# TensorE takes a mixer step one dense section ahead of the other engines in the feed-forward parts

## What is computed

```python
h = rmsnorm(x); u = h @ w_in
mix = concat(rglru(u), ssd(u), gated_delta(u), s5(u))   # four recurrent mixers
x = x + mix @ w_out
x = x + cross_attend(rmsnorm(x), mem_k, mem_v)
x = x + (silu(h2 @ w_gate) * (h2 @ w_up)) @ w_down       # h2 = rmsnorm(x), 2816 hidden
y = rmsnorm(x)
```

## Time and profile before

| | |
|---|---|
| median of 3 runs | 3927.91 us (3922.59 to 3929.86) |
| the profiled execution's own time | 3928.61 us |
| its span, first to last instruction | 3926.7 us |
| PE busy | 3555.5 us, 91% |
| PEld busy | 3385.3 us, 86% |
| DVE busy | 2189.3 us, 56% |
| ACT busy | 1349.6 us, 34% |
| mean granted TensorE clock | 0.949 |

### The profile page before, as it was taken

The page is one execution under the profiler, slowest core; times in us unless marked ns, Lnnn a source line. Parts: engine busy times, 40 slices in busy tenths (PEclk is TensorE's granted clock), DMA queues, the critical chain, the costliest instruction groups (busy, mean ns, idle before and its releaser), DMA issues.

```text
span 3926.7 us, 67616 instructions
## 1 busy us (share of the span) xinstructions
PE 3555.5 (91%) x26198; PEld 3385.3 (86%) x26198; DVE 2189.3 (56%) x4725; ACT 1349.6 (34%) x2497; POOL 97.1 (2%) x319
## 2 busy tenths in 40 slices
PE   6779796889879999889999998999998999989998
PEld 6778686678878999889899988899988899989998
DVE  6556754367855665663655572655573655554323
ACT  5553424244534343423332332322332432322101
POOL 2200001000000000000000000000000000000000
PEclk8979897889989999999999999999999999999999
DMA  7767567867686677667566667566668555566776
GB/s 222 235 228 252 191 213 246 240 209 241 234 283 246 245 276 265 249 237 259 194 229 217 211 236 282 188 230 221 217 220 281 187 203 189 204 236 237 250 252 212
DMA packets 370175, 909.58 MB, mean 232 GB/s; under 512 B 34368, under 2 KB 173248, under 8 KB 369472
## 3 DMA queue, kind: packets, MB, share of 16 engines
q1 hardware_dynamic: 369856, 905.26, 67.2%
HBM read 730.56 MB, written 174.57 MB: 231 GB/s over the span
## 4 chain that ended last, share of the span: by engine, by line
PE 49%; issue 19%; DVE 13%; DMA 6%; ACT 6%; DVEq 3%; SPq 2%; POOLq 1%; ACTq 1%; POOL 0%; PEldq 0%; PEld 0%
PE banks L479 14%; PE banks L480 13%; PE banks L481 13%; PE banks L1690 2%; DVE wlo_sb L1175 2%; DMA wlo_sb<-kept_dram 2%; ACT whi_sb L966 1%; DMA kept_dram<-wlo_sb 1%; DVE uc_sb L1267 1%; DVE m_p_sb L2297 1%; DVE m_p_sb L2267 1%; DVE hl_sb L1194 1%; DVE acc_sb L1184 1%; PE banks L1660 1%; DVE rstd_sb L1334 1%
## 5 line engine op out<-in xcount | busy, mean ns | idle before, releaser
L479 PE MATMUL banks<-hh_sb,whi_sb 128*128 128x384 f32 (+1 forms) x3360 | 1154.1, 343 | 98.1 <-DVE wlo_sb L1175 34.8
L480 PE MATMUL banks<-hh_sb,wlo_sb 128*128 128x384 f32 (+1 forms) x3360 | 1120.1, 333 | 0.0
L481 PE MATMUL banks<-hl_sb,whi_sb 128*128 128x384 f32 (+1 forms) x3360 | 1117.9, 333 | 0.0
L479 PEld LDWEIGHTS banks<-hh_sb,whi_sb 128*128 128x128 f32 x3360 | 650.7, 194 | 124.1 <-DVE wlo_sb L1175 43.2
L480 PEld LDWEIGHTS banks<-hh_sb,wlo_sb 128*128 128x128 f32 x3360 | 651.4, 194 | 1.6 <-issue 0.6
L481 PEld LDWEIGHTS banks<-hl_sb,whi_sb 128*128 128x128 f32 x3360 | 649.5, 193 | 0.0
L479 PE MATMUL banks<-g_hi_sb,whi_sb 128*128 128x384 f32 (+2 forms) x1504 | 516.4, 343 | 52.0 <-DVE x_sb L1380 21.5
L481 PE MATMUL banks<-g_lo_sb,whi_sb 128*128 128x384 f32 (+2 forms) x1504 | 501.8, 334 | 0.0
L480 PE MATMUL banks<-g_hi_sb,wlo_sb 128*128 128x384 f32 (+2 forms) x1504 | 501.6, 334 | 0.0
L1380 DVE TENSOR_TENSOR x_sb<-x_sb,banks 128x384 f32<-128x384 f32 (+2 forms) x400 | 201.3, 514 | 290.5 <-PE banks L481 274.7
L479 PEld LDWEIGHTS banks<-g_hi_sb,whi_sb 128*128 128x128 f32 x1504 | 294.9, 196 | 67.4 <-DVE x_sb L1380 25.2
(11 more groups left out here) (447 smaller groups left out, 4843.2 us busy)
## 6 DMA issues: line engine op xcount, KB each, us to landing
whi_sb<-kept_dram SPq DMA_DIRECT2D x504, 512.0 KB, 3.8
wlo_sb<-kept_dram SPq DMA_DIRECT2D x504, 512.0 KB, 4.9
raw_sb<-w SPq DMA_DIRECT2D x176, 512.0 KB, 5.0
kept_dram<-whi_sb SPq DMA_DIRECT2D x112, 512.0 KB, 5.3
kept_dram<-wlo_sb SPq DMA_DIRECT2D x112, 512.0 KB, 6.2
uc_dram<-uc_sb SPq DMA_DIRECT2D x90, 192.0 KB, 2.7
ldb_sb<-x_t SPq DMA_DIRECT2D x64, 192.0 KB, 4.6
plain_sb<-w SPq DMA_DIRECT2D x32, 256.0 KB, 5.0
```

Source lines behind the costliest of these rows:

```text
L479: eng.matmul(out, xh, yh, start=first, stop=False)
L480: eng.matmul(out, xl, yh, start=False, stop=False)
L481: return eng.matmul(out, xh, yl, start=False, stop=last)
```

## The change

`PE_PLAN` is a second plan, for PE alone. For each section `i` of kind `g`, `up` or `d` of a pass other than 0 that has a step behind it, PE takes one of its steps behind section `i - 1`, which is in front of section `i`. The other engines keep `PLAN`. The steps themselves, their waits and the sections are the same.

```diff
@@ -428,6 +428,19 @@
 PLAN = spread_over_windows()
+def ahead_on_pe():
+    plan = list(PLAN)
+    for i in range(1, len(SECS)):
+        if SECS[i].p and PLAN[i] and SECS[i].kind in ("g", "up", "d"):
+            plan[i] -= 1
+            plan[i - 1] += 1
+    return plan
+PE_PLAN = ahead_on_pe()
@@ -2879,11 +2892,11 @@
-        def weave(eng, section, mixer):
+        def weave(eng, section, mixer, plan=PLAN):
             mix = mixer(eng)
             for i in range(len(SECS)):
                 section(eng, i)
-                for _ in range(PLAN[i]):
+                for _ in range(plan[i]):
                     next(mix)
@@ -2892,7 +2905,7 @@
-            weave(pe, pe_section, pe_mixer)
+            weave(pe, pe_section, pe_mixer, PE_PLAN)
```

## The result

| | before | after |
|---|---|---|
| median (lowest to highest), 4 runs each | 3926.34 us (3922.59 to 3929.86) | 4151.98 us (4150.98 to 4161.36) |
| the profiled execution's own time | 3928.61 us | 4152.82 us |
| its span | 3926.7 us | 4150.9 us |
| mean granted TensorE clock | 0.949 | 0.942 |

The changed kernel is slower: the ratio after to before is 1.0584, with an interval of 1.0571 to 1.0596, which is 229 us; the medians lie 226 apart. From the planner on, the file is longer by 13 lines, so L1690 of before is L1703 of after, L2330 is L2343, L2349 is L2362, and so on.

What follows compares the result with a forecast made beforehand. PE was taken to bound the feed-forward parts of passes 1 to 4. Waits 201 - 24.5 given back + 36 clock = 212 us on 3928.6, so 4141, given as 4140 against the median; 8-in-10 range 4050 to 4250.

Steps and rivals of the forecast that it cites:

- Which waits: Of 122 moved steps with another step at section i-1, 106 make PE wait; 16 wait for ACT behind a d, priced at nothing.
- split by pass: The 122 steps with a step at i-1: 26 in each of passes 1 to 3, 44 in pass 4.
- Price of one: Each of 106 PE waits: section end to end of the needed DVE or ACT instruction, plus 0.15 us restart; 201 us.
- the rival of 4059 to 4100: Prices are smaller: the long steps shrink, giving 4059 us, or up to 4100 if only some do; chance 0.17.
- What it gives back: PE's five waits for g_lo and m_dec_x vanish, 18.3 us, plus 6.2 us of half clock behind four: 24.5 us.
- The clock: Half clock behind the longer PE waits in the feed-forward parts of passes 1 to 4: 29.5 + 7 = 36 us added.
- The rule: Clock charge per PE wait: nothing up to 1.6 us, half for nine at about 2, 1.55 us for 19 over 2.5.
- the stretch at 83 us: Trace evidence: waits of 0.8 to 1.6 us about every 4 us, 4.84 of 21 us idle, clock stayed at 1.00.
- The rival of the clock: Clock swings throughout the four stretches: the other 78 waits cost 1.55 us each too, 121 us, 4260 us; chance 0.15.
- near 0.9 in the stretches: Sign of being right: the granted clock near 0.9 in the feed-forward parts of passes 1 to 4.
- The length of the stretches: Sign of being right: each feed-forward part of passes 1 to 4 longer by 35 to 75 us, the fourth most.
- The rest of the span: Sign of being right: everything outside the feed-forward parts of passes 1 to 4 stays as before.

Runs made afterwards that it cites:

- The first experiment: All four engines, not PE alone, take the 192 steps one section earlier, against the kernel before: 3914.36 us, ratio 0.9986.
- the free moves: Only the 79 steps priced at nothing are moved one section earlier on PE, against the kernel before: 3931.82 us, ratio 1.0025.
- the double eviction: The changed kernel with DVE evicting each g and up of passes 1 to 4 twice: 4267.2 us, ratio 1.0886 to before.
- the third: The changed kernel with 128 of the 384 columns of each g and up eviction of passes 1 to 4 done twice: 4217.41 us, ratio 1.0751 to before.
- the first four experiments: Against before: all engines ahead, 3914.36 us; on PE alone, 79 steps priced at nothing, 3931.82; steps 6 to 18, 4040.88; the other 66, 4015.46.
- the mirror: PE alone takes the 192 steps one section later than in the kernel before: 4065.68 us, ratio 1.0366.
- before with the double eviction: The kernel before with DVE evicting each g and up of passes 1 to 4 twice: 3944.97 us, ratio 1.0055.
- the one with seven steps later: The kernel before with PE alone taking seven steps one section later, six in u sections and one at an up: 3916.56 us, ratio 0.998.

## Why the prediction was right

4140 us was forecast and 4152 measured, by the mechanism that was named and nearly at its price. Point by point:

- **Which waits.** 106 of 122 were to wait and 16 not; the trace shows just these. The first experiment confirms the cause: with the others' steps moved along, PE's list unchanged, none of the 106 but one waits for over 0.3 us (2.5 us, for an `m_dec` that was late in before too). The prediction's split by pass was misread, 26, 26, 26 and 44 where the plan has 25, 25, 25 and 47; the sum of 122 is right, and no price hangs on the split.
- **Price of one.** 201 us predicted, 203.1 in the trace. The kinds agree one by one. The mean idle time, to which the restart comes, was 1.1 to 1.3 us at steps 6, 8 (the three behind an `up` with L1280 first 2.1, priced at 2.2), 10, 12, 14, 16, 17 and 19 (predicted 1.3 with the restart), 1.4 to 1.5 at 7, 9, 11 and 13 (1.6), 1.97 at 15 (2.1), 2.96 at 4 (3.0), 4.3 at 20 behind an `up` (4.65), 3.54 at 1 (3.65) and 4.34 at 2 (4.4). Off were step 5, with one wait of 3.0 in place of 1.55, and step 20, 0.2 less than priced behind an `up` and 0.5 behind a `d`. That DVE and ACT would shrink their long steps with the idle time that they gained (the rival of 4059 to 4100) did not happen: 106 waits are one eviction and one step long, and none of either can start before the bank is full.
- **What it gives back.** 24.5 us were booked, and only part came. DVE's waits for PE inside the levels are gone from the FFN parts, as was said (L2347 for L1690 there: 20.4 us in 37 before, none in after). `g_lo` holds PE for 4.6 us in place of 18.5 over the whole kernel. The row of `m_dec` rose from 21.3 to 25.9 all the same, but not as a new name for `g_lo`: its two waits of pass 4 (2.6 and 2.8 us) are now at the moved step 2, 4.35 each, which the prices have. Idle time other than that of the moved steps went from 30.4 to 203.1 - 185.9 - 1.9 = 15.3 us, so 15 of the 18.3 us of idle time came back. In the kernel with only the free moves they did not: there the wait for `g_lo` turned into one for `m_dec_x`.
- **The clock.** +36 less 6 were booked. Half-clock busy grew by 73.2 us; at the pitches of rows 12 that is 73.2 x (1 - 0.17/0.32) = 34 us. By class, in the table above: nothing for waits up to 1.6 us, as priced; 5.1 us for the nine at about 2, priced at 7; 25.2 for the 19 over 2.5, priced at 29.5. The rule held in each of its parts, and half for the nine was near the truth in kind too: 4 of them lose and 5 don't. That waits up to 1.6 us are free was well guessed rather than read: of the five waits in the stretch at 83 us only one is over 1 us. What the rule left out is what lies between 1.6 and 2 us. In after that is five waits, in the kernels with the longer eviction 24 and 37, and I had expected those to be as free as at 1.2: the double eviction should have cost 51 us and a little, and it cost 119.
- **The rival of the clock** had 0.15: four stretches with the clock swinging throughout, 4260. In after the clock is 0.97 to 0.99 in three of the stretches and 0.94 in the fourth. The Trainium skill, "TensorE: Matmul & The Clock Gate", section "A second HAM failure mode: psum-queue depth-cycling", says that short idle times between groups of products, when frequent, make the clock go back and forth. The runs bear it out only above a length: the 57 waits of 1 to 1.6 us, frequent as they are, cost no clock, and when a longer eviction carried most of them past 1.6 us they did (the sections behind these 57 lose 18 us with the third and 31 with the double). The sign "near 0.9 in the stretches" was wrong, and it doesn't follow from the prediction's own +36 either: at 1.55 us lost for 3.3 us of half clock that is 77 us of it in some 1600, a mean near 0.97.
- **The length of the stretches.** 35 to 75 us each, the fourth most, was forecast; it was 41, 41, 41 and 96. The order was right and the fourth mis-sized: it holds 43 of the 106 waits, 79.1 us of their 185.9, and 51.2 of the 109.3 us that the four parts spend at half clock, idle time in them included.
- **The rest of the span.** "As before" was right to 5 us. In it, two waits changed: `hl` L1205 rose from 1.2 us to 16.4, and that for the DMA of `wlo` fell from 50.7 to 36.9.

The place of the loss, its mechanism and the part of the step prices are shown by the trace and by the first four experiments. That the loss at half clock grows with the length of the waits is shown by three doses; that the length alone decides is not shown, see the last section. Open are, besides, which steps make up the mirror's 144 us and why its weights are late, where the 10 us of the free moves lie, and why before with the double eviction loses 22 us, where at most 12 were expected (its FFN parts hold 11 us more of idle time and are 13 longer together; the rest is outside them).

## What to carry to other kernels

When an engine's list is moved by one place against the others', the price of each waiting step can be read beforehand: from the end of the section on the bound engine to the end of the instruction that it needs, along the list of the engine that makes it, with everything queued ahead of it, here one eviction of 0.56 us. The slack of that engine doesn't help, since it is idle before the eviction and not behind it; the test for the idea is to move all lists together, which here cost nothing and gained 0.1%. A wait that goes away is booked as a gain only once the next late instruction behind it is known: in two kernels here, the one with the free moves and the one with seven steps later, it came back under another name.

## What the runs showed of the hardware

In these runs the share of the waits that cost clock grew with their length, and it grew within a narrow range. PE could wait 57 times for 1 to 1.6 us, in sections of some 4 us, and the sections behind lost nothing; with a third of an eviction more in front, 24 waits were 1.6 to 2 us long, and 14 of the sections behind lost 0.7 to 1.6 us each. So half-clock busy went from 102 to 177 and 225 us with some 0.3 and 0.6 us more in each wait behind a `g` or an `up`, at a mean granted clock of 0.942, 0.937 and 0.932 over the whole execution. I had not expected a few tenths of a microsecond to cost as much in clock as in waiting.

Nor is the length all that decides. In the kernel with a third more, the six waits of step 13 are 1.90 us long; five of the sections behind lose about 1.5 us and one loses nothing. With the double, the eight waits of step 12 are 1.84 us long and cost nothing, while two of the eight of step 6, just as long, cost 0.8 and 1.0. What else decides, the waits and the work just before among it, no run here tells apart.
